# Other pads between the late buffers: gated buffers 32 and 224 bytes, the arena 64 bytes off, modulo 256

## What is computed

```python
def _conv_ffn(h, w_up, conv_w, conv_b, w_down):
    u = _causal_dwconv(h @ w_up, conv_w, conv_b)      # w_up: 1024 x 5632
    a, b = jnp.split(u, 2, axis=-1)
    return (jax.nn.gelu(a) * b) @ w_down              # w_down: 2816 x 1024
```

## Time and profile before

| | us |
|---|---|
| three runs | 1259.56, 1260.03, 1262.29 |
| median | 1260.03 |
| the profiled execution | 1264.54 |
| its span, first to last instruction | 1263.2 |
| PE busy in it | 1219.7 |
| DVE busy | 900.7 |
| ACT busy | 609.6 |

### The profile page before, as it was taken

How to read it: one execution, slowest core, us unless ns; L and a number is a source line. 1 busy time by engine, 2 the same in 40 slices (tenths; PEclk the granted TensorE clock), 3 DMA queues, 4 the chain that set the end, 5 groups by cost and what they waited for, 6 DMA issues and landing times. The chain is left out here.

```text
span 1263.2 us, 21186 instructions
## 1 busy us (share of the span) xinstructions
PE 1219.7 (97%) x8525; PEld 1117.1 (88%) x8528; DVE 900.7 (71%) x1266; ACT 609.6 (48%) x919; POOL 108.0 (9%) x148
## 2 busy tenths in 40 slices
PE   7999999999999999999999999999998999999997
PEld 5888888987899999889988899998986899999996
DVE  4876997574667888855668767777665598666677
ACT  2242213452656666734665555555414464555552
POOL 2894000003000000001000000000200000000000
PEclk8999999988999999999999999999999799999999
DMA  9544443533745666615425357668345204565561
GB/s 275 172 134 130 138 134 134 172 118 120 237 153 164 221 226 213 220 50 169 149 77 177 126 199 231 216 212 198 101 141 165 75 1 168 168 199 198 183 216 39
DMA packets 178734, 202.76 MB, mean 161 GB/s; under 512 B 21884, under 2 KB 163163, under 8 KB 178636
## 3 DMA queue, kind: packets, MB, share of 16 engines
q1 hardware_dynamic: 175083, 191.49, 47.5%
q0 software_dynamic: 3184, 9.77, 2.5%
q10 hardware_dynamic: 369, 0.13, 0.1%
HBM read 200.30 MB, written 1.08 MB: 159 GB/s over the span
## 5 line engine op out<-in xcount | busy, mean ns | idle before, releaser
L1483 DVE TENSOR_TENSOR w_parts<-raw,w_parts 128x1024 fp32r<-128x1024 f32 (+1 forms) x242 | 294.9, 1219 | 123.5 <-ACT w_parts L1472 118.1
L1766 PEld LDWEIGHTS ps<-hT_parts,w_parts 128*128 128x128 f32 x2880 | 332.3, 188 | 3.2 <-DVE w_parts L1483 1.0
L1766 PE MATMUL ps<-hT_parts,w_parts 128*128 128x256 f32 x2880 | 334.5, 277 | 0.4 <-DVE w_parts L1483 0.3
L1472 ACT CAST w_parts<-raw 128x1024 fp32r<-128x1024 f32 (+1 forms) x242 | 253.4, 1047 | 159.1 <-PE ps L1766 54.3
L478 PE MATMUL ps<-hT,ring 128*128 128x256 f32 x448 | 100.3, 385 | 1.0 <-DVE hT L321 1.0
L1536 PE MATMUL ps<-hT_parts,w_parts 128*128 128x256 f32 x816 | 98.6, 281 | 2.4 <-DVE w_parts L1483 1.5
L1536 PEld LDWEIGHTS ps<-hT_parts,w_parts 128*128 128x128 f32 x816 | 96.4, 189 | 3.1 <-DVE w_parts L1483 1.7
L478 PEld LDWEIGHTS ps<-hT,ring 128*128 128x128 f32 x448 | 85.7, 193 | 14.3 <-issue 1.6
L1890 DVE SCALAR_TENSOR_TENSOR arena_late<-ps,vecT,arena_late 128x255 f32<-128x255 f32 (+1 forms) x176 | 84.9, 482 | 11.0 <-ACT arena_late L1840 4.7
L1785 PE MATMUL ps<-w_parts,g0T_parts 128*128 128x512 f32 x360 | 87.3, 398 | 1.3 <-DVE w_parts L1483 1.3
L1785 PE MATMUL ps<-w_parts,g1T_parts 128*128 128x512 f32 x360 | 86.9, 395 | 0.0
(11 more groups left out here) (417 smaller groups left out, 1618.1 us busy)
## 6 DMA issues: line engine op xcount, KB each, us to landing
raw<-in_ffn_w_up SPq DMA_DIRECT2D x44, 1024.0 KB, 5.1
raw<-in_f_w_up SPq DMA_DIRECT2D x22, 1024.0 KB, 5.2
raw<-in_ffn_w_down SPq DMA_DIRECT2D x22, 1024.0 KB, 5.0
ring<-in_w_in SPq DMA_DIRECT2D x18, 1024.0 KB, 5.4
raw<-in_ev_w_in SPq DMA_DIRECT2D x15, 1024.0 KB, 5.5
raw<-in_f_w_down SPq DMA_DIRECT2D x11, 1024.0 KB, 5.0
ring<-in_x_wkv SPq DMA_DIRECT2D x8, 1024.0 KB, 5.4
ring<-in_w_out SPq DMA_DIRECT2D x4, 1024.0 KB, 8.0
```

Of the source, the lines that this page charges most:

```text
L1472: self.done(A, A.copy(high[:, c], self.raw[:, u % RAW, c]), self.s_hi)
L1483: self.done(V, V.tensor_tensor(low[:, c], self.raw[:, u % RAW, c], high[:, c].bitcast(F32), ALU.subtract), self.s_lo)
L1766: mm = T.matmul(self.ps[:, b, m * 256:m * 256 + 256], w[:, kk, m * P:(m + 1) * P], x[:, kk, :], start=kk == 0 and q == 0, stop=kk == KD - ...
```

## The change

Three pads get other sizes. In bytes, the pad before `g0T_parts` goes from 160 to 96, the one before `g1T_parts` from 64 to 192, and the one before the arena from 288 to 160. No instruction is added, removed or moved on any engine.

```diff
         self.hTr = self.sb("hT_parts", [P, 2, KD, SEQ], F32R)[:, :, :, :]
         self.gTr = []
-        for i, pad in enumerate((40, 16)):
+        for i, pad in enumerate((24, 48)):
             self.sb(f"pad_g{i}", [P, pad])
             self.gTr.append(self.sb(f"g{i}T_parts", [P, 2, 2, SEQ], F32R))
-        self.sb("pad_arena", [P, 72])
+        self.sb("pad_arena", [P, 40])
         self.arena_cols = 26624 - 256
```

## The result

The changed kernel is slower. Its median is 1265.27 us over 11 runs, against 1261.15 for the kernel before over 11; the ratio is 1.0038 with a 95% interval of 1.0028 to 1.0049, some 5 us. The forecast was 1257.0 with a range of 1253.0 to 1262.5: the wrong sign, and outside the range.

The account below looks back on a forecast made before the run. The prediction took PE, busy for 97% of the span, to bound the kernel through its matmuls' pitch. Its terms, -2.4-0.5-0.1 = -3.0 us, took the median of 1260.0 to 1257.0 us, with a range of 1253.0 to 1262.5.

Parts of the forecast that it names:

- Part 1: 660 matmuls of lines 1732 and 2179 over `parts` get a cheaper pitch at distance 64 instead of 0: -2.4 us.
- Part 2: 240 matmuls of line 1536 after the first feed-forward stage may take over the 113.6 ns pitch: -0.5 us.
- The premise from the earlier trace: yM with w0, then w1, kept its pitch level of 113.6 ns over an unbroken change of buffers.
- Part 3: 720 matmuls of 512 columns loading the gated buffers change pitch: -0.1 us, bounds -1.9 to +2.6 us.
- Part 4: Stretches of line 1766 entered behind `pe_down` keep their pitch of 113.6 ns: 0 us.
- The rival: Line 1766 falls to the higher level, 117.7 ns: +9.4 us for 2300 matmuls, time 1266.4 us; chance 0.12.

Follow-up runs that it names:

- the arena alone: Against the kernel before, only the arena moves, to 128 bytes from `w_parts` modulo 256, gated buffers as before: 1258.22 us, ratio 0.998.
- g0 alone: Against the kernel before, the arena moves to 128 and g0 to 32, g1 stays at 160: 1257.47 us, ratio 0.9971.
- the probe: Kernel before with unread matmuls added at its end, loading and streaming at places every 16 bytes modulo 256; its total time was read for nothing.

## Why the prediction was wrong

- **Part 1, the places aside: right.** -2.4 us forecast from a middle between the levels. Measured pitches of 115.6 and 114.2 ns, both levels among them; -2.7 us by pitch in the changed kernel, and a ratio of 0.998 with the arena alone. There is some luck in the size: which level a stretch takes was not known, and with the arena at 128 the mean of line 1732 over `parts` went from 114.5 to 115.6 ns from trace to trace.
- **Part 2, the projection behind them: wrong by its 0.5 us.** Line 1536 stayed at 117.8 in the changed kernel. There the aside units ahead of it ended at 117.8 too. But in the other seven kernels with the arena at 128 they ended at 113.4, and all 240 matmuls behind them still ran at 117.8. So a low level is not handed over at this border. The two rows are from the kernel with g0 alone, (2320-276)/18 = 113.6 and (2280-281)/17 = 117.6:

```profile
560.25 2.32 PE L1732 MATMUL ps<-parts,hT_parts 128*128 128x256 f32 x19
...
563.80 2.28 PE L1536 MATMUL ps<-hT_parts,w_parts 128*128 128x256 f32 x18
```

The premise from the earlier trace rows doesn't hold either. In the changed kernel's execution yM with w0 ran at 117.8 ns and went down to 113.4 as soon as w1 took over, with the same places as before.
- **Part 3, the gated buffers' own pitch: right.** -0.1 us forecast, -0.3 measured. The bounds were not: 512 columns go down to 227 ns, not 231, as the probe shows. Reading the 256-column rows for 512 columns was a mistake of kind: d = 0 is nearly the worst for one and nearly the best for the other.
- **Part 4, the entry into line 1766: the step that failed.** It took 0 on the ground that behind `pe_down`'s last matmul both operands lie where they did. That looked at the one pair at the border. The runs show that the level behind it hangs on the gated buffers' places: with g1 at 224 instead of 160 and all else alike, the mean of line 1766 went from 113.66 ns (g0 alone) to 116.95 (the changed kernel), +8.9 us against before. How the 24 matmuls ahead of the border pass that on is open. Every entry known before had been behind 96 or 160, two places behind which the level was low whatever came in; both are in the prediction as two differing places with one outcome, and two were too few.
- **The rival was right in the line, the level and the price.** It said +9.4 us for 2300 matmuls at 4.1 ns. The trace has some 2300 at the high level, about 300 of which had been there before, and +8.9 us by the mean pitches. It said 1266.4, and the median is 1265.27. That close a hit is partly luck: the rival meant +6.4 us over 1260.0, while the ratio gives +4.8 over the 1261.15 us of the kernel before. It had 0.12, and the range was cut at 1262.5, in the middle of it. A level known to have two values, on a line with 2880 matmuls, deserved more than that: its price was three times that of all other terms together.
- What the prediction worked out from the Trainium skill (TensorE: Matmul & The Clock Gate, Part 2, on PE's two independent read ports), that no place can matter, did not come true; the prediction went by the rows instead. The runs disagree with it too: the placing of buffers alone moved the time between 1254.7 and 1265.9 us.

## What to carry to other kernels

Where PE is the bound and loads and streams fp32r operands all the time, the places of the two operands modulo 256 bytes are worth some 1% of the time, and can be set by pads. Here that was 1254.7 against 1265.9 us. Measure the pitch from start to start, since durations hardly move. Don't choose a place by the pitch of its own matmuls: look at what the stretch behind them runs at, since the place may decide the level of the next stretch. A level seen behind two places says little about a third, and a table from an isolated probe has to be tried in the kernel: 16 and 192 did there what the probe had not shown. When a term is a state with two levels, sum it over all that would take it, and let the range reach to that sum.

## What the runs showed of the hardware

- In the probe, after a fresh start, matmuls with fp32r operands of 256 columns that load the activations ran at 113.4 ns from start to start at a distance of 64 bytes (loaded less streamed, modulo 256), and at 116.7 to 120.2 at all other multiples of 16. With 512 columns it was 226.7 to 229.5 ns at 176, 192, 240, 0 and 16, and 231.9 to 234.4 elsewhere. No run moved a buffer by 256 bytes alone, so that 256 is the period is not shown by itself.
- The same matmuls at the same places can settle at either of two pitches: 113.6 or 117.8 ns for 256 columns, in both forms; 229.4 or 233.3 for 512 columns with both gated buffers at 192. A stretch of line 1766 settles within its first six or so matmuls and mostly keeps the level to its end. Where one changed for good in the first stage (six of the ten traces of the kernel and its variants), it did so at a pause of some 200 to 230 ns between its two halves.
- Counted over the ten traces, by the pitch of the matmuls 9 to 20 of a stretch, all 72 stretches behind line 1785 at 96 or 160 were low, 11 of them with a high one ahead. All 36 behind 224 were high, 17 of them with a low one ahead, and so were all 24 behind 0, 6 of them with a low one ahead. The probe agrees at all four. Behind 32 all 41 with a low one ahead were low; with a high one ahead 18 were high and one was low, and the probe's was low. Behind 192 all 21 with a low one ahead were low; with a high one ahead two were high and one was low, and the probe's was low. At 16 low and high alternated. In the probe alone, 64 turned the level over and 128 kept it.
- Behind aside units at 113.4 ns line 1536 ran at 117.8, in seven traces: a change of form and buffer without a gap can end the low level.
- Why it is so, by which banks or buffers of the memory, no run here tells.
